# The last norm of block one and the first norm of block two done as one, token transposes early, last picks one by one

## What is computed

```python
def first_block(x, c, ...):
    mod = silu(c) @ w_ada + b_ada              # six vectors of 1024
    hmix = rmsnorm(x, norm_mix_w) * (1 + scale1) + shift1
    proj = hmix @ w_in                         # conv, window attention, gated delta, gates ga and gb
    ...
    x = x + gate2 * experts(...)
    return rmsnorm(x, final_norm_w)            # the last norm of block one

def second_block(x, ...):
    h = rmsnorm(x, norm1_w)                    # the first norm of block two
    x = x + mixers(h) @ w_out
    h = rmsnorm(x, norm2_w)
    for each token, for each of its 128 picks i with gate g_i:
        y += gelu(h . u[idx_i]) * g_i * v[idx_i]
    return x + y
```

## Time and profile before

| | us |
|---|---|
| median of 3 runs | 1695.36 |
| lowest, highest | 1693.72, 1697.14 |
| the profiled execution, its time | 1694.07 |
| the profiled execution, its span | 1692.2 |
| busy in the span: TensorE / VectorE / ScalarE / GpSimd | 1475.6 / 784.0 / 265.1 / 308.1 |
| mean transfer rate over the span | 325 GB/s |

### The profile page before, as it was taken

The page is one execution under the profiler, slowest core; times in us unless marked ns, Lnnn a source line. Parts: engine busy times, 40 slices in busy tenths (PEclk is TensorE's granted clock), DMA queues, the critical chain, the costliest instruction groups (busy, mean ns, idle before and its releaser), DMA issues.

```text
span 1692.2 us, 16785 instructions
## 1 busy us (share of the span) xinstructions
PE 1475.6 (87%) x6282; PEld 800.6 (47%) x6282; DVE 784.0 (46%) x1830; ACT 265.1 (16%) x644; POOL 308.1 (18%) x288
## 2 busy tenths in 40 slices
PE   4999999599999999999699798898777777787877
PEld 2897885444444444443446575553333333333333
DVE  2116754513232322322333466376766666676553
ACT  1312221100000000000033321222212121212111
POOL 0001000100000000000000012355444444444440
PEclk8999999699999999999899899999999999889999
DMA  9532347389999999999405138799999999999994
GB/s 376 226 108 96 147 150 298 130 344 427 428 428 427 426 423 427 427 429 428 203 33 216 51 137 304 305 376 422 421 422 421 421 422 421 422 421 421 421 422 200
DMA packets 60273, 551.06 MB, mean 326 GB/s; under 512 B 8608, under 2 KB 8896, under 8 KB 10400
## 3 DMA queue, kind: packets, MB, share of 16 engines
q1 hardware_dynamic: 22192, 277.47, 39.7%
q0 software_dynamic: 38000, 272.50, 39.4%
HBM read 548.90 MB, written 1.05 MB: 325 GB/s over the span
## 4 chain that ended last, share of the span: by engine, by line
PE 47%; DMA 39%; issue 5%; DVE 5%; POOL 2%; ACT 2%; SPq 0%; DVEq 0%; POOLq 0%; ACTq 0%
DMA ring<-peer_uv_d,work 19%; DMA ring<-expert_w_d 14%; PE ps L1462 9%; PE ps L1120 7%; PE ps L1712 7%; DMA consts_sb<-peer_uv_d,work 5%; PE ps L1212 5%; PE ps L1114 5%; PE ps L1571 4%; PE ps L1502 2%; PE ps L1451 1%; PE ps L1369 1%; DMA ring<-w_ada_d 1%; POOL ring L1845 1%; PE ps L1473 1%
## 5 line engine op out<-in xcount | busy, mean ns | idle before, releaser
L1712 PE MATMUL ps<-ring,work 128*128 128x512 f32 x752 | 364.6, 637 | 92.5 <-ACT work L1063 92.5
L2726 DVE CUSTOM_DVE_ANT_0 ring<-ring,work 128x1024 f32<-128x1024 f32 x188 | 229.8, 1223 | 134.8 <-DMA ring<-peer_uv_d,work 133.1
L1712 PEld LDWEIGHTS ps<-ring,work 128*128 128x128 f32 x752 | 149.3, 204 | 301.9 <-issue 178.9
L1845 POOL DMA_INDIRECT ring<-peer_uv_d,work x188 | 205.7, 1094 | 269.1 <-PE ps L1712 180.1
L1462 PE MATMUL ps<-ring,work 128*64 128x512 f32 x1024 | 226.6, 597 | 9.3 <-DMA ring<-expert_w_d 8.5
L1462 PEld LDWEIGHTS ps<-ring,work 128*64 128x64 f32 x1024 | 77.9, 138 | 154.8 <-issue 153.6
L1120 PE MATMUL ps<-ring,hT 128*128 128x512 f32 (+1 forms) x288 | 123.0, 586 | 1.7 <-issue 0.8
L1063 ACT ACTIVATE work<-consts_sb,work 128x128 f32<-128x128 f32 x256 | 82.3, 390 | 266.4 <-DVE work L2734 263.2
L1502 PE MATMUL ps<-ring,work 128*64 128x512 f32 x512 | 113.4, 595 | 0.7 <-DVE work L2356 0.7
L1712 PE MATMUL ps<-work 128*128 128x512 f32 x136 | 78.0, 703 | 39.9 <-ACT work L1063 39.9
L2352 DVE TENSOR_TENSOR work<-work,ps 128x512 f32<-128x512 f32 x16 | 11.0, 688 | 199.1 <-PE ps L1462 199.1
(11 more groups left out here) (388 smaller groups left out, 1502.3 us busy)
## 6 DMA issues: line engine op xcount, KB each, us to landing
ring<-expert_w_d SPq DMA_DIRECT2D x96, 2048.0 KB, 15.7
ring<-w_in_d SPq DMA_DIRECT2D x13, 2048.0 KB, 18.0
ring<-w_ada_d SPq DMA_DIRECT2D x12, 2048.0 KB, 8.1
ring<-w_out_d SPq DMA_DIRECT2D x4, 2048.0 KB, 8.0
ring<-peer_w_query_d SPq DMA_DIRECT2D x4, 2048.0 KB, 7.7
ring<-peer_uv_d,work POOLq DMA_INDIRECT x188, 23.4
mod<-b_ada_d SPq DMA_DIRECT2D x1, 2048.0 KB, 26.8
consts_sb<-consts_d SPq DMA_DIRECT2D x1, 1346.0 KB, 26.4
```

The lines of the kernel that those rows point to most:

```text
L1712: last = pe.matmul(ps[V_BANK[t] + n][:, :], diag[:, i % 4, :], v_row(i)[:, n * 512:(n + 1) * 512], start=(i % (16 * PH) == 0), stop=(i % ( ...
L1845: pool.indirect_dma_start(out=uv_rows(i), out_offset=None, in_=io["peer_uv"], in_offset=bass.IndirectOffsetOnAxis(ap=idx[:, s, k:k + 1], a ...
L2726: dve.tensor_tensor_reduce(out=u_row(i), in0=u_row(i), in1=h_tok[:, i // (16 * PH), :], scale=1.0, scalar=0.0, op0=ALU.mult, op1=ALU.add, ...
```

## The change

Three edits in one.

First, the head. The four transpose jobs come first, before the ada tiles, and are emptied without scale and shift (by plain copies); scale and shift are applied in place, hT to hT, chunks 0 to 4 on VectorE and 5 to 7 on ScalarE, once mod_t is there. The column sums of tile n are made behind tile n+1; eight 128x128 matmuls whose result nobody reads (`warm`) stand behind each of the first three tiles. The gate columns (`gab`) move behind k1 on TensorE and VectorE. All later jobs of block one take the next bank.

Second, the two norms. With m = mean((x w)^2) r^2 for the mean square of the first norm's result, h_tok = (x w) r s mod, with r and s the two inverse roots. VectorE makes x w (into h_tok) and x's sum of squares, ScalarE the sum of squares of x w. Tile 0 goes through to its `tok_ready` before tile 1 is begun; tile 1's steps and the scaling of x itself, for both tiles, follow behind the copy of tile 0's second transposes. `nw_used` is raised by two behind that.

Third, the picks. The last eight are batches of one; the weights of the last batch of four are issued behind the first dot of the eight, and each single's behind its own dot. In the last `result` the first bank is waited for by itself (`half_done`).

```diff
-    jobs = [("ada0", 0, "D"), ("ada1", 1, "D"), ("ada2", 0, "D"), ("ada3", 1, "D"), ("col", 2, "D"),
-            ("xT0", 4, "D"), ("xT1", 5, "D"), ("xT2", 6, "A"), ("xT3", 7, "A"), ("gab", 3, "D")]
+    jobs = [("xT0", 4, "D"), ("xT1", 5, "D"), ("xT2", 6, "A"), ("xT3", 7, "A"), ("ada0", 0, "D"), ("ada1", 1, "D"),
+            ("ada2", 0, "D"), ("ada3", 1, "D"), ("col", 2, "D")]
...
+def batches(n):
+    return [(i, BATCH) for i in range(0, n - 8, BATCH)] + [(i, 1) for i in range(n - 8, n)]
+PICKS = batches(16 * TT * PH)
...
+            for g in (2, 3):
+                act.activation(hT[:, 2 * g:2 * g + 2, :], halves(done(f"xT{g}")), ACT.Copy).then_inc(ev_a, 1)
             act.wait_ge(mod1_ready, 1)
...
+            for k in (5, 6, 7):
+                act.activation(hT[:, k, :], hT[:, k, :], ACT.Identity, scale=mod_t[:, 8 + k:9 + k],
+                               bias=mod_t[:, k:k + 1]).then_inc(hx_a, 1)
...
+            def weighted_sums(t):
+                act.wait_ge(xw_ready, t + 1)
+                act.activation(acc[:, 1, :], h_tok[:, t, :], ACT.Square, scale=D ** -0.5,
+                               accum_out=ms[:, 2 + t:3 + t]).then_inc(xw_sums, 1)
...
+            for n in range(N_ADA1):
+                b = hbank(f"ada{n}")
+                hfull(condition(b, head_tile("ada", n)))
+                if n:
+                    columns(n - 1)
+                if n < N_ADA1 - 1:
+                    warm(8)
+            hbank("col")
+            hfull(columns(N_ADA1 - 1))
+            pe.wait_ge(hx_d, 5)
+            pe.wait_ge(hx_a, 3)
...
+                if name == "k":
+                    gate_columns()
...
+            def both_norms(t):
+                r, s, m = rstd[:, t:t + 1], rstd[:, 2 + t:3 + t], ms[:, 2 + t:3 + t]
+                rooted(t)
+                dve.wait_ge(xw_sums, t + 1)
+                o(dve.scalar_tensor_tensor(m, m, r, r, ALU.mult, ALU.mult))
+                post(root_in)
+                rooted(2 + t)
+                o(dve.tensor_tensor(s, s, r, ALU.mult))
+                sync()
+                dve.wait_ge(in_nw3, 16)
+                o(dve.scalar_tensor_tensor(h_tok[:, t, :], h_tok[:, t, :], s, mod[:, 0, :], ALU.mult, ALU.mult))
+                post(tok_ready)
...
+            weighted(0)
+            own_sums(0)
+            both_norms(0)
...
+            weighted(1)
             features_in("nT", 0, 1)
+            own_sums(1)
+            both_norms(1)
+            for t in range(TT):
+                o(dve.scalar_tensor_tensor(x[:, t, :], x[:, t, :], rstd[:, t:t + 1], nw[:, :], ALU.mult, ALU.mult))
+            sync()
+            dve.sem_inc(nw_used, 2)
...
-                if i >= 2 * BATCH and i % BATCH == 1:
+                if i >= 2 * BATCH and i % BATCH == 1 and i < 16 * N_STEP - 8:
                     weights(i // BATCH - 1)
+                if i == 16 * N_STEP - 8:
+                    weights((16 * N_STEP - 8) // BATCH - 1)
+                if i >= 16 * N_STEP - 8:
+                    weights((16 * N_STEP - 8) // BATCH + i - (16 * N_STEP - 8))
```

132 lines of the change are left out of this document (74 added, 58 removed).

## The result

| | before | changed |
|---|---|---|
| median, us | 1696.25 | 1677.53 |
| single runs, us | 1693.72, 1695.36, 1697.14, 1699.99 | 1674.56, 1674.69, 1680.37, 1680.74 |
| the profiled execution, its time and span | 1694.07, 1692.2 | 1674.69, 1672.9 |
| busy: TensorE / VectorE / ScalarE / GpSimd | 1475.6 / 784.0 / 265.1 / 308.1 | 1473.3 / 786.6 / 269.7 / 305.4 |

The ratio is 0.9892, with a 95% interval of 0.9868 to 0.9917: the change is faster by 18.7 us, and 1677.5 lies in the forecast range, 1.5 above the value named. The busy times say little about it again: TensorE has 2.3 us less, GpSimd 2.7 less, VectorE and ScalarE a few more. The 18.7 us were taken out of three waits.

What follows compares the result with a forecast made beforehand. Transfers bound the experts and picks, so only work before or after them counts: head 5.6 + between blocks 5.4 + tail 7.7 = 18.7 us off 1694.07 gives 1675.4, said as 1676; own range 1671 to 1680, overall 1669 to 1684.

Steps and rivals of the forecast that it cites:

- Transposes and column sums: Head: transposes start at about 10.9; four sums remain after the last ada tile, ending at 32.5, 4.0 us earlier.
- k0 at 35.3: Head: the first projection starts at 35.3 (range 35.1 to 36.0), 10.5 us earlier; after 37 would show it wrong.
- they cost nothing while that cover holds: Head: 24 filler matmuls fit between ada tiles, 4.7 us per round in the 5.0 of a tile's arrival; otherwise under 1 us.
- Modulation, 1.7 us: Head: scale and shift read hT in SBUF; bounds 0.9 and 2.4 us on VectorE, ScalarE 1.5; 1.7 taken.
- The clock, first fall in k0, second at the gate columns: Head: k0 still starts at low clock; gate columns can drop it again for q0, 0 to 1.7 us, 0.8 taken off.
- Head 5.6: Start of block one, up to the projections: net gain 5.6 us, ends 3.5 (both clock falls long) and 9 (none).
- Between the blocks, 5.4: From the experts' last add to block two's first transpose: tile 0's norms first and joined save 5.4 us (4.5 to 5.7).
- Tail 7.7: Last picks: TensorE works on without a pause, ending at 1681.3 instead of 1688.2; with the split sum 7.7 us (6.2 to 9.2).
- Head absorbed: Rival: something later in block one gives back the head's 5.6 us before the experts' transfers; gain 13.1, 1682; chance 0.15.
- nothing moves: Rival: the three gains are hidden, above all because another engine sets the pick stretch's start; within 0.2%; chance 0.04.
- Slower: Rival: the clock does not return through the six projections (35 to 85 us), costing 41 us, about 1717; chance 0.04.
- Low clock: Rival: clock down through k0 and q0, block two and tail start in a worse phase; gain 14.5, about 1680; chance 0.16.

Runs made afterwards that it cites:

- e6: The changed kernel with the gate columns put back ahead of k0; median 1677.88 us, ratio 0.9896 to the kernel before.
- e1: The kernel before with only the new head's edits; median 1687.36 us, ratio 0.9942.
- e5: The changed kernel without the 24 unread filler matmuls between the ada tiles; median 1680.55 us, ratio 0.9901 to the kernel before.
- e9: The changed kernel with fillers regrouped (5, 5, 4 between tiles, ten ahead of k0) and the last sixteen picks single; median 1670.69 us, ratio 0.9852.
- e10: The changed kernel with ten more unread matmuls ahead of TensorE's first transposes; median 1677.23 us, ratio 0.9898 to the kernel before.
- e8: The changed kernel with 26 unread matmuls between the experts and block two; median 1682.26 us, ratio 0.9920 to the kernel before.
- e4: The changed kernel again with no edit, measured beside its three parts; median 1673.06 us, ratio 0.9865 to the kernel before.
- e3: The kernel before with only the new last picks; median 1688.67 us, ratio 0.9956.

## Why the prediction was right

The time (1676.0 forecast, 1677.5 measured), the sign and the mechanism of all three parts hold. That the gain is 18.7 us in both is luck in part: the second measurement of the same kernel gives 22.6, and in the profiles a head that is worth more than forecast, 1.8 us lost behind it and 0.9 us gained on the way to the last dot nearly cancel. By the steps:

- **Transposes and column sums.** The transposes start at 11.22, as forecast. The sums end at 33.97, forecast 32.5. That is not their price: the last ada tile landed at 30.03, where it had landed at 28.68, and the steps behind it take 3.9 us (30.03 to 33.97) as forecast (28.68 to 32.5, 3.8).
- **k0 at 35.3** (range to 36.0, wrong if after 37): 36.5, all by that landing. e6 shows the same steps without it: tile at 28.77, and TensorE goes on behind the modulation at 35.26. With the old head the tile landed at 28.5 to 28.8 in all profiles that show it; with the new one at 28.6 to 29.0 in e1, e5, e6 and e9, and at 29.9 to 30.4 in six others. The forecast had no term for it; it costs 1.2 to 1.7 us where it occurs. The landing records show what it is: the tile comes in sixteen parts, and in the changed kernel fifteen have landed by 28.64 and the last at 30.03. In all six the one part is late, in e10 already that of the third tile (25.05 after 23.51). The packets marked as instruction point to the cause. In these six a 16 KB packet starts at 22.9 (e10) or between 26.9 and 27.9, while the tile is on its way; in e5 and e9, with fewer of TensorE's instructions ahead, the first such packet comes at 32.6, and with the old head at 35.7 to 38.0. So the 24 unread matmuls seem to have moved a load of TensorE's code into the arrival of the tile. It isn't shown: e1 and e6 have the packet too (27.5 and 27.9) and no late part.
- **The fillers, "they cost nothing while that cover holds".** A round of tile, sums and fillers took 4.73 us (19.21 to 23.94; 4.7 forecast), so the price was right. But the first tiles were taken late: in the changed kernel they landed at 13.66, 18.55 and 23.45 and TensorE began them 1.1, 0.7 and 0.5 us later, because the transposes ran until 14.87. That is the sign of being wrong that the prediction named; by the fourth tile it was made up (the fillers ahead of it ended at 28.74). In e1, whose transposes began at 12.2, it was not: the fourth tile landed at 29.04 and was begun at 30.22, and k0 started at 36.6 all the same.
- **Modulation, 1.7 us.** 1.72 on VectorE, 1.58 on ScalarE. The SBUF price was the right row to be near. The rule of the Trainium skill that I had named beside it ("VectorE: DVE Perf Modes", Mode 2x_2P, both read ports from SBUF) agrees in direction: 0.34 us for 256 elements from SBUF, 0.48 from PSUM.
- **Gate columns, 4.1 back.** 3.5, at full clock behind k1.
- **The clock, first fall in k0, second at the gate columns.** The first fall was there, as forecast. The second was not in the changed kernel's profile, and was in e1, e8 and e9 (the columns took 4.53, 4.30 and 4.50 us): it comes in some executions. The forecast of 0.8 for a fall that costs 0 or more was fair.
- **Head 5.6.** In the two profiles it is 6.5 us at ss; by the runs of e1 it is 8.3. This is the term that was mis-sized, and the failure is not in the steps of the new head but in the price of the old one: I took one profile of before as its price, although its own median lay above that execution. The old head's ss lies between 89.8 and 95.1 in four profiles. Part of the head's worth is that it takes the place of work whose clock is uncertain. The rest of the surplus is lost on the way: in the changed kernel's profile 1.8 us between ss and the experts, where e4, the same kernel, loses nothing (249.0 and 246.7).
- **Between the blocks, 5.4.** Measured 5.4. TensorE starts 5.7 us after VectorE's first operation, forecast 5.6. ScalarE's square took 1.06 and 0.19 to read out, hidden, with no table load in the way. The cover for tile 1's work held. What I had not seen is that TensorE itself needs most of the remaining 7.2 us, though the record of its branch (6.30 us) stands in the profile of before.
- **Tail 7.7.** 7.8 in the stretch by these two profiles; by the runs of e3 7.0, and by the spread of the stretch in all profiles between 4.0 and 7.8. That spread comes from the clock in an earlier batch, which the forecast had only in its range (6.2 to 9.2). End of TensorE 5.5 us after the last dot's start forecast, 5.3 measured; the bound by the last dot was put at 1.5 us less, and e9 found 1.2. The sign held: TensorE's longest idle time in the last 20 us is 0.34. The early start of the result's first half gives the 0.8.
- **The rivals.** "Head absorbed" and "nothing moves" are out: experts and picks take the same time within 2 us in all profiles, and what is gained ahead of them arrives. The first indirect load starts 11.0 us earlier than before, 11.0 forecast for head and norms, and the picks run at 421 GB/s as before. "Slower" by a clock that doesn't return is out: it was back within 4 us. "Low clock" is partly there, in executions: the runs at 1680.4 and 1680.7 lie where this rival was put. Neither was profiled, so this is not shown.
- **The rule on transposes.** I had weighed the sentence of the Trainium skill ("TensorE: Matmul & The Clock Gate", the transpose mode) that transposes in that mode don't count as busy in the same way, and had said that the trace disagrees. That was more than its rows give: before, the column sums ran until 36.5, directly ahead of the transposes. In the changed kernel the first ada tile takes 2.50 us right behind 3.65 us of transposes, between the 3.64 of the low and the 1.92 of the high clock: the clock rose within it. e10, with ten plain matmuls in front, has 2.53 for the transposes and 1.92 for the tile. Neither settles the rule: the rise came after transposes and the tile's first matmuls together.
